# Two of an expert's six weight pieces loaded as one transfer with 32 KB rows

## The chip, the cores and the metric
One core of a Trainium2 chip runs the whole program as one launch. The metric is the device time of an execution in microseconds (us), the lower the better; three executions give a median.

## The reference
A decoder layer for 256 tokens of width 1024, all in float32: RMS norm and a projection, two groups of mixing heads (attention with forgetting, RWKV-7), an output projection, then a mixture of experts, then a gated per-layer input and a last norm. The expert part, cut to what matters here:

```python
logits = xt @ w_router + b_router
top_val, top_idx = lax.top_k(logits, 4)          # 4 of 32 experts for each token
gates = jax.nn.softmax(top_val, axis=-1)
# for each block of tokens that share an expert e:
hh = xb @ w_gu[e] + b_gu[e]                      # 1024 x 2048 weights, 8 MB
glu = jnp.minimum(hh[:, :1024], 7.0)
lin = jnp.clip(hh[:, 1024:], -7.0, 7.0)
act = glu * jax.nn.sigmoid(1.702 * glu) * (lin + 1.0)
out += (act @ w_down[e] + b_down[e]) * gate      # 1024 x 1024 weights, 4 MB
```

## The kernel before
The mixing part takes the first 240 us. After it, the kernel works through items: an item is one expert with up to 64 of its tokens. There are 32 items in this execution (3072 matmul records of line 855 stand for 32 items of 6 pieces of 16 records), numbered 0 to 31; how many there are is known only at run time.

**Pieces.** The weights of an item, 12 MB, are cut into six pieces of 2 MB, each with 128 rows of 16 KB, one row for each partition. Pieces 0 to 3 are the gate and up matrices, pieces 4 and 5 the down matrix. In HBM all lie in one array `we[expert, piece]`. In SBUF there are nine places: `ring` has six slots, one for each piece, and `extra` (the tile B) has three more for pieces 3, 4 and 5 of odd items. So pieces 0 to 2 have one place each, and pieces 3 to 5 have two each, for even and odd items.

**TensorE.** `item` (line 864) runs on TensorE: biases, then `product` for pieces 0, 1, 2, 3, then the scatter of the former item (L832), the gate matrix (L879), transposes of the activation (L899), the gather for item i + 2 (L817), product 4, transposes of gathered tokens (L824), product 5. The next item begins with its biases (L869). `product` (line 844) waits for the landing semaphore of its piece and then issues its matmuls (L855); the last of them counts up `s_used`. So `s_used` is 6 i + q + 1 when piece q of item i has been used.

**SyncE.** It issues every weight load, in the order of its program, on one queue, and waits for `s_used` ahead of each, so that the place is free. `first_item` (L337) loads item 0; lines 364 and 372 load pieces 3 to 5 of item 1, and line 387 its pieces 0 to 2 and pieces 3 to 5 of item 2. Then two loops follow. `ahead` (line 404), for items 2 to 9: pieces 0 to 2 of item i, then pieces 3 to 5 of item i + 1, each once the same piece of item i - 1 has been used. `in_turn` (line 411), from item 10 on: the six pieces of item i in their order, pieces 0 to 2 once item i - 1 has used them, pieces 3 to 5 once item i - 2 has. After item 31 come the gate weights of the tail (`wgate`, L428, two pieces of 2 MB into ring slots 3 and 4) and the final gain.

**The tail** after item 31: a last scatter (L840), transposes (L935), the gate products (L941), activation, norm and the stores.

Of the kernel before, what the change touches and what calls it, by code (L numbers as in the profile page):

```python
# [18 lines left out]
D = 1024  # L19
# [121 lines left out]
def fox_rwkv7_moe_ple(nc, t, out):  # L141
    with ExitStack() as ctx:
# [3 lines left out]
        def sem(name):  # L146
            return ctx.enter_context(nc.semaphore(name))
# [3 lines left out]
        ring = sb("ring", [P, NSLOT, KD * PW])  # L151
# [4 lines left out]
        B = sb("B", [P, 15, D])  # L156
# [103 lines left out]
        s_bt = sem("expert_bias_landed")  # L260
        s_we = [sem(f"expert_piece{q}_landed") for q in range(6)]
        s_odd = [sem(f"odd_expert_piece{q}_landed") for q in range(3, 6)]
        s_ple = sem("layer_projection_landed")
# [8 lines left out]
        s_used = sem("expert_pieces_used")  # L272
# [46 lines left out]
        def _(sp):  # L319
# [7 lines left out]
            for n in range(NSLOT):  # L327
                piece(n, t[f"wz{n}"], ZP[n][1])
                if n == 1:
# [4 lines left out]
                    sp.dma_start(brt[:, :], t["brt"]).then_inc(s_aux, 16)  # L334

            def first_item(q):
                sp.dma_start(ring[:, q, :], t["we"][0, q]).then_inc(s_we[q], 16)  # L337

# [32 lines left out]
            sp.wait_ge(s_dve, dve_at["mix"])  # L371
            sp.dma_start(extra[2], t["we"][1, 5]).then_inc(s_odd[2], 16)
            sp.wait_ge(s_pe, pe_at["xo10"])
# [4 lines left out]

            def place(q, odd):
                return extra[q - 3] if odd and q >= 3 else ring[:, q, :]  # L380

            def landed(q, odd):
                return s_odd[q - 3] if odd and q >= 3 else s_we[q]

            for q in range(6):
                sp.wait_ge(s_used, q + 1)
                sp.dma_start(place(q, q < 3), t["we"][1 if q < 3 else 2, q]).then_inc(landed(q, q < 3), 16)

# [5 lines left out]
            last_pair = pairs + 1  # L394
            EARLY = 4
# [3 lines left out]

            def load(e, q, odd):  # L400
                sp.dma_start(place(q, odd), t["we"][bass.ds(e, 1), q, :, :].rearrange("a p n -> (a p) n"))\
                    .then_inc(landed(q, odd), 16)
# [8 lines left out]
            def in_turn(i, odd, qs=range(6)):  # L411

                e = weights(i)
                for q in qs:
                    sp.wait_ge(s_used, 6 * i + (q - 5 if q < 3 else q - 11))
                    load(e, q, odd)

            with sp.Fori(0, EARLY) as p:
                ahead(2 * p + 2, False)
                ahead(2 * p + 3, True)  # L420
            in_turn(2 * EARLY + 2, False, range(3))
            in_turn(2 * EARLY + 3, True)
            with sp.Fori(EARLY, pairs) as p:
                in_turn(2 * p + 4, False)
                in_turn(2 * p + 5, True)
            for q in range(2):
# [19 lines left out]
        def _(pe):  # L446
# [396 lines left out]

            def product(i, odd, q, bank_, lhs, first):
                weights = extra[q - 3] if odd and q >= 3 else ring[:, q, :]
                w = weights.rearrange("p (k h c) -> p k h c", k=4, h=2)
                if q < 3:
                    pe.wait_ge(s_we[q], 16 * i + 16)
                elif odd:
                    pe.wait_ge(s_odd[q - 3], 8 * i + 8)  # L850
                else:
                    pe.wait_ge(s_we[q], 8 * i + 16)
# [9 lines left out]
            x_of, act_of = half_of(xT), half_of(aT)  # L862

            def item(i, odd, first=False, last=False):
# [17 lines left out]
                for q in range(4):  # L882
                    if last and q == 3:
                        former()
                        gate_matrix()
                    product(i, odd, q, 6 + q // 2, x_of, False)
                    if first and q < 3:
                        (overflow_rows, overflow_places, overflow_tables)[q]()
# [14 lines left out]
                pe.wait_ge(s_aT, i + 1)  # L903
                product(i, odd, 4, 4, act_of, True)
                if not last:
# [14 lines left out]
            last_pair = pairs + 1  # L920
# [806 lines left out]
```

## Time and profile before

| | us |
|---|---|
| median of three executions | 1198.04 |
| lowest and highest | 1197.19 to 1199.14 |
| the profiled execution | 1197.98 |
| its span, first to last instruction | 1196.2 |
| TensorE busy | 1140.5 |
| DMA, time that the packets of the load queue took, share of 16 engines' span | 86.5% |

The profile is of one execution. The span is 1.8 us shorter than the time of that execution. A busy time of TensorE means matmuls in flight, and SyncE (SP) counts as a queue of issues: the row of an issue has its start and how long the issuing took, and how long the transfer took to land stands separately.

### The profile page before, as it was taken

To read this page: it belongs to the slowest core of one execution; us is meant where nothing else is said; L and a number is where in the kernel's file an instruction comes from. 1 tells how busy PE (TensorE), PEld (TensorE's weight loads), DVE (VectorE), ACT (ScalarE), POOL (GpSimd) and SP (SyncE) were. 2 spreads that over 40 slices of the span, in tenths; PEclk is the share of its full clock that TensorE was granted. 3 is DMA by queue.
4 is the path that set the end of the run, shared out by engine and by line. 5 is a ranking of instruction groups with operands and counts; after the bars stand their busy time and mean duration, and the time that the engine had idled before them with its cause. 6 is when DMAs were issued, how large, how long until landed. Compare 5 with 4: busy or idle time off the path is not lost.

```text
span 1196.2 us, 16921 instructions
## 1 busy us (share of the span) xinstructions
PE 1140.5 (95%) x7060; PEld 482.8 (40%) x7060; DVE 282.4 (24%) x576; ACT 173.1 (14%) x319; POOL 0.2 (0%) x4
## 2 busy tenths in 40 slices
PE   7999999999999999999999999999999999999997
PEld 6888866533333333333333333333333333333334
DVE  2455635321111211111211211111111111111123
ACT  3323432210100100000010010000000000000015
POOL 0000000000000000000000000000000000000000
PEclk9999999899999999999999999999999999999999
DMA  9732125579999999999999999999999999999970
GB/s 378 316 141 73 44 101 212 228 292 393 429 427 429 429 428 428 429 428 428 429 428 428 429 428 430 428 428 429 428 428 428 428 429 429 428 428 429 427 332 36
DMA packets 32228, 434.90 MB, mean 364 GB/s; under 512 B 3840, under 2 KB 4096, under 8 KB 5952
## 3 DMA queue, kind: packets, MB, share of 16 engines
q1 hardware_dynamic: 32192, 434.37, 86.5%
q8 instruction: 29, 0.48, 0.2%
q14 instruction: 7, 0.06, 0.0%
HBM read 433.31 MB, written 1.05 MB: 363 GB/s over the span
## 4 chain that ended last, share of the span: by engine, by line
DMA 42%; PE 40%; DVE 1%; issue 0%; ACT 0%; SPq 0%; DVEq 0%
DMA ring<-in_we 42%; PE PS L855 27%; PE PS L941 2%; PE PS L703 2%; PE PS L817 2%; PE PS L832 2%; PE PS L869 1%; PE PS L824 1%; PE PS L753 1%; PE PS L899 0%; PE PS L879 0%; PE PS L759 0%; PE PS L731 0%; PE PS L498 0%; DVE xq L1248 0%
## 5 line engine op out<-in xcount | busy, mean ns | idle before, releaser
L855 PE MATMUL PS<-ring,FV 128*64 128x512 f32 x2304 | 515.4, 596 | 26.1 <-DMA ring<-in_we 26.1
L855 PEld LDWEIGHTS PS<-ring,FV 128*64 128x64 f32 x2304 | 158.0, 137 | 364.6 <-issue 302.1
L855 PE MATMUL PS<-B,FV 128*64 128x512 f32 x768 | 174.0, 595 | 9.4 <-DMA B<-in_we 8.7
L855 PEld LDWEIGHTS PS<-B,FV 128*64 128x64 f32 x768 | 53.0, 137 | 114.4 <-issue 98.6
L486 PE MATMUL PS<-hT,ring 128*128 128x256 f32 x416 | 93.0, 382 | 0.9 <-ACT hT L994 0.7
L486 PEld LDWEIGHTS PS<-hT,ring 128*128 128x128 f32 x416 | 78.1, 190 | 12.3 <-ACT hT L994 0.8
L1475 DVE TENSOR_SCALAR rz<-con,lora 64x64 f32<-64x64 f32 x30 | 7.4, 247 | 306.1 <-PE PS L855 306.1
L1557 DVE TENSOR_SCALAR hT<-PS 128x512 f32<-128x512 f32 x32 | 22.1, 692 | 185.7 <-PE PS L855 185.7
L1248 DVE TENSOR_TENSOR FV<-PS,prm 128x512 f32<-128x512 f32 x32 | 22.1, 692 | 184.6 <-PE PS L824 184.6
L1153 ACT ACTIVATE FV<-PS 128x512 f32<-128x512 f32 x32 | 19.1, 597 | 298.4 <-PE PS L899 298.4
L817 PE MATMUL PS<-xq,rz 128*64 128x512 f32 x256 | 62.0, 605 | 0.0
L832 PE MATMUL PS<-B,rz 64*128 64x512 f32 x248 | 61.6, 615 | 0.0
L1151 ACT ACTIVATE hT<-hT 128x512 f32<-128x512 f32 x32 | 20.1, 630 | 270.2 <-DVE hT L1549 270.2
L1157 ACT ACTIVATE B<-PS 128x512 f32<-128x512 f32 x32 | 19.1, 597 | 224.4 <-PE PS L855 224.4
L832 PEld LDWEIGHTS PS<-B,rz 64*128 64x128 f32 x248 | 21.4, 186 | 39.7 <-issue 39.7
L869 PE MATMUL PS<-FG,rz 32*64 32x512 f32 x256 | 34.8, 612 | 0.9 <-DVE FV L1248 0.9
L941 PE MATMUL PS<-ring,hT 128*128 128x512 f32 (+1 forms) x80 | 28.1, 508 | 0.2 <-DVE hT L1248 0.2
L703 PE MATMUL PS<-ring,hT 128*128 128x512 f32 x64 | 28.1, 592 | 0.0
L1248 DVE TENSOR_TENSOR hT<-hT 128x512 f32<-128x512 f32 x32 | 22.2, 693 | 21.7 <-ACT hT L1151 21.6
L817 PEld LDWEIGHTS PS<-xq,rz 128*64 128x64 f32 x256 | 15.5, 136 | 24.9 <-issue 23.4
L1139 ACT ACTIVATE B<-PS 128x512 f32<-128x512 f32 x32 | 19.1, 597 | 41.5 <-PE PS L817 41.5
L1549 DVE TENSOR_SCALAR hT<-PS 128x512 f32<-128x512 f32 x32 | 21.6, 676 | 10.4 <-PE PS L855 10.4
(264 smaller groups left out, 679.4 us busy)
## 6 DMA issues: line engine op xcount, KB each, us to landing
ring<-in_we SPq DMA_DIRECT2D x144, 2048.0 KB, 24.2
B<-in_we SPq DMA_DIRECT2D x48, 2048.0 KB, 29.3
ring<-in_wz SPq DMA_DIRECT2D x7, 2048.0 KB, 22.7
ring<-in_wo SPq DMA_DIRECT2D x2, 2048.0 KB, 7.9
ring<-in_wgate SPq DMA_DIRECT2D x2, 2048.0 KB, 38.7
xq<-in_x SPq DMA_DIRECT2D x2, 512.0 KB, 5.4
ring<-in_wz SPq DMA_DIRECT2D x1, 1024.0 KB, 8.6
xq<-in_x SPq DMA_DIRECT2D x1, 1024.0 KB, 5.0
```

The lines of the kernel that those rows point to most:

```text
L486: mm = pe.matmul(bank(z_bank(n), SEQ), w[:, k, at:at + P], hT[:, k, :], **flags)
L703: mm = pe.matmul(bank(2 * q + b), mixT[:, k, b * P:(b + 1) * P], w[:, k, :], start=(k == 0), stop=(k == KD - 1))
L817: mm = pe.matmul(PS[64 * h:64 * h + 64, 6, :], PM[:, b, :], xs[:, b, 512 * h:512 * h + 512], start=(b == 0), stop=(b == TB - 1))
L832: mm = pe.matmul(bank(2 * q + b), GTs[rows, b * P:(b + 1) * P], ysb[rows, :], start=False, stop=False, skip_group_check=True)
L855: mm = pe.matmul(PS[64 * h:64 * h + 64, bank_, :], lhs(4 * (q % 2) + k), w[:, k, h, :], start=(first and k == 0), stop=(q % 2 == 1 and k = ...
L869: pe.matmul(PS[64 * h:64 * h + 64, 6 + s, :], OHB[NE * s:NE * s + NE, :], bT[NE * s:NE * s + NE, 512 * h:512 * h + 512], start=True, stop= ...
L941: mm = pe.matmul(PS[:, 2 * q + b if c0 == 0 else 4, 0:c1 - c0], hT[:, k, b * P:(b + 1) * P], w[:, k, c0:c1], start=(k == 0), stop=(k == KD ...
L1139: act.activation(Xg, bank(6), ACT.Copy).then_inc(s_xg, 1)
L1151: act.activation(e_s, e_g, ACT.Sigmoid, scale=SALPHA).then_inc(s_sig, 1)
L1248: return v.tensor_tensor(o, a, b, op)
L1549: v.tensor_scalar(e_g, bank(6), LIMIT, None, ALU.min).then_inc(s_glu, 1)
L1557: v.tensor_scalar(e_l, bank(7), LIMIT, -LIMIT, ALU.min, ALU.max).then_inc(s_vl, 1)
```

## The change
The arrays in HBM are split: `we0`, `we1`, `we2` and `we5` hold one piece each, and `we34` holds pieces 3 and 4 of each expert side by side, so that a row is 32 KB. Where a merged load is made, one transfer of 4 MB fills both places (ring slots 3 and 4, or the first two places of `extra`), on one semaphore. It is issued once piece 4 of the former owner has been used (before, piece 3 waited for piece 3, and piece 4 for piece 4), and product 3 waits for all of it. It is done for item 1 and for items 3 to 30. Items 0 and 2 and the last item keep single transfers (`last_in_turn`), which read half rows of `we34`. For items 0 and 2 pieces 3 and 4 share a semaphore, and product 3 waits for both. The loops keep their order of loads; `in_turn` is split so that the last item stands behind the loop. The core of the diff (the renamed semaphores and the host's concatenation are left out):

```diff
+        extra34 = B[:, 0:8, :].rearrange("p a n -> p (a n)")
...
             sp.wait_ge(s_pe, pe_at[f"y{NC - 1}"])
-            for a in range(2):
-                sp.dma_start(extra[a], t["we"][1, 3 + a]).then_inc(s_odd[a], 16)
+            sp.dma_start(extra34, t["we34"][1]).then_inc(s_odd[0], 16)
...
+            ring34 = ring[:, 3:5, :].rearrange("p a n -> p (a n)")
+            def up(e, i):
+                for q in range(3):
+                    sp.wait_ge(s_used, 6 * i + (q - 5))
+                    sp.dma_start(ring[:, q, :], of(t[f"we{q}"], e)).then_inc(s_up[q], 16)
+            def down(e, i, odd, used):
+                sp.wait_ge(s_used, 6 * i + (used + 5))
+                sp.dma_start(extra34 if odd else ring34, of(t["we34"], e)).then_inc((s_odd if odd else s_down)[0], 16)
+                sp.wait_ge(s_used, 6 * i + (used + 6))
+                sp.dma_start(extra[2] if odd else ring[:, 5, :], of(t["we5"], e)).then_inc((s_odd if odd else s_down)[1], 16)
             def ahead(i, odd):
                 e, e_next = weights(i), weights(i, 1)
-                for q in range(6):
-                    sp.wait_ge(s_used, 6 * i + (q - 5))
-                    load(e if q < 3 else e_next, q, odd == (q < 3))
+                up(e, i)
+                down(e_next, i, not odd, -6)
+            def in_turn(i, odd):
                 e = weights(i)
-                for q in qs:
-                    sp.wait_ge(s_used, 6 * i + (q - 5 if q < 3 else q - 11))
-                    load(e, q, odd)
+                up(e, i)
+                down(e, i, odd, -12)
+            def last_in_turn(i):
+                e = weights(i)
+                up(e, i)
+                for a in range(2):
+                    sp.wait_ge(s_used, 6 * i + (a - 8))
+                    sp.dma_start(extra[a], of(t["we34"][:, :, 4 * D * a:4 * D * (a + 1)], e)).then_inc(s_last4 if a else s_odd[0], 16)
+                sp.wait_ge(s_used, 6 * i - 6)
+                sp.dma_start(extra[2], of(t["we5"], e)).then_inc(s_odd[1], 16)
...
-            in_turn(2 * EARLY + 2, False, range(3))
-            in_turn(2 * EARLY + 3, True)
+            up(weights(2 * EARLY + 2), 2 * EARLY + 2)
             with sp.Fori(EARLY, pairs) as p:
+                in_turn(2 * p + 3, True)
                 in_turn(2 * p + 4, False)
-                in_turn(2 * p + 5, True)
+            last_in_turn(2 * last_pair + 1)
...
                 elif odd:
-                    pe.wait_ge(s_odd[q - 3], 8 * i + 8)
+                    if last and q == 4:
+                        pe.wait_ge(s_last4, 16)
+                    else:
+                        pe.wait_ge(s_odd[q // 5], 8 * i + 8)
```

## Rows read from the trace of the kernel before

**Rows 1.** The page: TensorE, rates in 40 slices of 29.9 us, the chain by engine.
```profile
PE 1140.5 (95%) x7060; PEld 482.8 (40%) x7060; DVE 282.4 (24%) x576; ACT 173.1 (14%) x319; POOL 0.2 (0%) x4
...
GB/s 378 316 141 73 44 101 212 228 292 393 429 427 429 429 428 428 429 428 428 429 428 428 429 428 430 428 428 429 428 428 428 428 429 429 428 428 429 427 332 36
...
DMA 42%; PE 40%; DVE 1%; issue 0%; ACT 0%; SPq 0%; DVEq 0%
```

**Rows 2.** Busy time by stretch; last columns: TensorE clock, DMA share, GB/s.
```profile
400.00:534.00 134.00, 125.67 (x596) 40.64 (x592) 22.58 (x51) 10.84 (x19) 0.00 (x0) 1.00 1.01 428
543.00:690.00 147.00, 147.00 (x712) 49.85 (x712) 27.17 (x61) 13.90 (x23) 0.00 (x0) 1.00 1.01 429
729.00:1136.00 407.00, 381.87 (x1804) 124.59 (x1804) 68.65 (x150) 33.27 (x55) 0.00 (x0) 1.00 1.01 428
```

**Rows 3.** Chain in order of time, items 29 to 31: start, us, what.
```profile
1081.24 25.49 DMA ring<-in_we
1106.77 3.68 PE PS L855 x16
1110.60 25.49 DMA ring<-in_we
1136.13 3.65 PE PS L855 x16
```

**Rows 4.** TensorE in order of time, items 3 to 5: nothing waits for a load.
```profile
337.50 3.60 PE L855 MATMUL PS<-B,FV 128*64 128x512 f32 x16
341.03 1.99 PE L832 MATMUL PS<-B,rz 64*128 64x512 f32 x8
...
354.24 13.96 PE L855 MATMUL PS<-ring,FV 128*64 128x512 f32 x64
...
381.34 10.52 PE L855 MATMUL PS<-ring,FV 128*64 128x512 f32 x48
391.69 0.60 PE L855 MATMUL PS<-B,FV 128*64 128x512 f32 x2
```

**Rows 5.** TensorE in order of time, late items: products 2 and 3 of 30.
```profile
1106.77 3.65 PE L855 MATMUL PS<-ring,FV 128*64 128x512 f32 x16 [0.58 <-DMA ring<-in_we]
1111.67 3.65 PE L855 MATMUL PS<-ring,FV 128*64 128x512 f32 x16 [1.25 <-DMA ring<-in_we]
```

**Rows 6.** Chain of the tail, then issue and landing of the gate weights.
```profile
1148.69 7.09 PE PS L855 x32
...
1161.15 3.67 PE PS L941 x8
...
1192.39 0.75 DVE xq L1615
...
L428 SPq DMA_DIRECT2D ring<-in_wgate x2: 338/342/346, 1115.4 to 1123.4; - x2
...
DMA to landing us min/median/max: 37.2/38.7/40.3
```

**Rows 7.** Packets in 11:12 (16 KB rows), 185:186 (8 KB rows), 600:700; page: x again.
```profile
q1 hardware_dynamic: 24, 0.39, 91.7%
...
q1 hardware_dynamic: 54, 0.44, 104.3%
...
DMA packets 2947, 42.85 MB, mean 428 GB/s; under 512 B 332, under 2 KB 332, under 8 KB 332
...
q1 hardware_dynamic: 2947, 42.85, 100.6%
...
xq<-in_x SPq DMA_DIRECT2D x1, 1024.0 KB, 5.0
```

**Rows 8.** Issues of SyncE, each with its landing, then all loads of weights.
```profile
283.65 0.33 SPq L401 DMA_DIRECT2D ring<-in_we  x1
...
DMA to landing us min/median/max: 15.5/15.5/15.5
...
295.14 0.33 SPq L401 DMA_DIRECT2D B<-in_we  x1
...
DMA to landing us min/median/max: 7.5/24.8/38.4
```

**Rows 9.** Items 13 and 14: issue and landing of a piece 4, TensorE after product 3.
```profile
593.35 0.33 SPq L401 DMA_DIRECT2D B<-in_we  x1
...
DMA to landing us min/median/max: 24.0/24.0/24.0
...
622.47 1.99 PE L832 MATMUL PS<-B,rz 64*128 64x512 f32 x8
```

**Rows 10.** Busy time by stretch, the end of the mixing part.
```profile
229.80:236.60 6.80, 6.80 (x16) 3.54 (x15) 2.18 (x12) 0.54 (x3) 0.00 (x0) 0.50 0.77 325
236.70:245.00 8.30, 7.36 (x37) 2.57 (x38) 3.80 (x17) 2.85 (x4) 0.00 (x0) 1.00 0.00 0
```

More of the change, by code:

```diff
@@ L260, in fox_rwkv7_moe_ple @@
         s_bt = sem("expert_bias_landed")
-        s_we = [sem(f"expert_piece{q}_landed") for q in range(6)]
-        s_odd = [sem(f"odd_expert_piece{q}_landed") for q in range(3, 6)]
+        s_up = [sem(f"expert_piece{q}_landed") for q in range(3)]
+        s_down = [sem("expert_pieces34_landed"), sem("expert_piece5_landed")]
+        s_odd = [sem("odd_expert_pieces34_landed"), sem("odd_expert_piece5_landed")]
+        s_last4 = sem("last_expert_piece4_landed")
         s_ple = sem("layer_projection_landed")
@@ L334, in _, with single @@
                     sp.dma_start(brt[:, :], t["brt"]).then_inc(s_aux, 16)
+            def single(q):
+                if q in (3, 4):
+                    return t["we34"][:, :, (q - 3) * 4 * D:(q - 2) * 4 * D]
+                return t[f"we{q}"]
             def first_item(q):
-                sp.dma_start(ring[:, q, :], t["we"][0, q]).then_inc(s_we[q], 16)
+                sp.dma_start(ring[:, q, :], single(q)[0]).then_inc(s_up[q] if q < 3 else s_down[q // 5], 16)
             def after(n):
@@ L371, in _ @@
             sp.wait_ge(s_dve, dve_at["mix"])
-            sp.dma_start(extra[2], t["we"][1, 5]).then_inc(s_odd[2], 16)
+            sp.dma_start(extra[2], t["we5"][1]).then_inc(s_odd[1], 16)
             sp.wait_ge(s_pe, pe_at["xo10"])
@@ L377, in _ @@
             first_item(5)
[L379 to L383, printed above, removed]
             for q in range(6):
                 sp.wait_ge(s_used, q + 1)
-                sp.dma_start(place(q, q < 3), t["we"][1 if q < 3 else 2, q]).then_inc(landed(q, q < 3), 16)
+                sp.dma_start(ring[:, q, :], single(q)[1 if q < 3 else 2]).then_inc(s_up[q] if q < 3 else s_down[q // 5], 16)
             sp.wait_ge(s_used, 7)
@@ L398, in weights, with of @@
                 return sp.value_load(EI[0:1, bass.ds(i + a, 1)], min_val=0, max_val=NE - 1)
-            def load(e, q, odd):
-                sp.dma_start(place(q, odd), t["we"][bass.ds(e, 1), q, :, :].rearrange("a p n -> (a p) n"))\
-                    .then_inc(landed(q, odd), 16)
+            def of(w, e):
+                return w[bass.ds(e, 1), :, :].rearrange("a p n -> (a p) n")
+            ring34 = ring[:, 3:5, :].rearrange("p a n -> p (a n)")
[8 more added lines that the diff above has]
+                sp.dma_start(extra[2] if odd else ring[:, 5, :], of(t["we5"], e)).then_inc((s_odd if odd else s_down)[1], 16)
             def ahead(i, odd):
                 e, e_next = weights(i), weights(i, 1)
-                for q in range(6):
-                    sp.wait_ge(s_used, 6 * i + (q - 5))
-                    load(e if q < 3 else e_next, q, odd == (q < 3))
-            def in_turn(i, odd, qs=range(6)):
+                up(e, i)
+                down(e_next, i, not odd, -6)
+            def in_turn(i, odd):
                 e = weights(i)
-                for q in qs:
-                    sp.wait_ge(s_used, 6 * i + (q - 5 if q < 3 else q - 11))
-                    load(e, q, odd)
+                up(e, i)
[8 more added lines that the diff above has]
+                sp.dma_start(extra[2], of(t["we5"], e)).then_inc(s_odd[1], 16)
             with sp.Fori(0, EARLY) as p:
@@ L842, in scatter_last, with product @@
                     finish(mm, "tpe", f"s{b}")
-            def product(i, odd, q, bank_, lhs, first):
+            def product(i, odd, q, bank_, lhs, first, last=False, head=False):
                 weights = extra[q - 3] if odd and q >= 3 else ring[:, q, :]
@@ L885, in item @@
                         gate_matrix()
-                    product(i, odd, q, 6 + q // 2, x_of, False)
+                    product(i, odd, q, 6 + q // 2, x_of, False, last, first)
                     if first and q < 3:
@@ L903, in item @@
                 pe.wait_ge(s_aT, i + 1)
-                product(i, odd, 4, 4, act_of, True)
+                product(i, odd, 4, 4, act_of, True, last, first)
                 if not last:
@@ L1712 @@
     dn = a["w_down"][0].reshape(NE, 2, 4, P, D).transpose(0, 1, 3, 2, 4).reshape(NE, 2, P, 4 * D)
-    host["we"] = np.concatenate([gu, dn], 1)
+    for q in range(3):
+        host[f"we{q}"] = gu[:, q]
+    host["we34"] = np.concatenate([gu[:, 3], dn[:, 0]], -1)
+    host["we5"] = dn[:, 1]
     host["bT"] = np.concatenate([a["b_gu"][0][:, 0:FF], a["b_gu"][0][:, FF:]], 0)
```

8 lines of the change are left out of this document (6 added, 2 removed).

## The prediction
> **What bounds the kernel now.** I read the page first, then the stretches, the chain, the two engines in order of time and the packets.
>
> The page shows TensorE busy for 95% of the span and a load rate of 427 to 430 GB/s in nearly every slice from the eleventh to the thirty-eighth [rows 1]. The two bounds lie so close together that the share of busy time doesn't settle which one holds. The stretches do. Between 400 and 534 us and between 729 and 1136 us TensorE is idle for 8.3 and 25.1 us, with the rate at 428 GB/s; between 543 and 690 us it is never idle, at the same rate [rows 2]. So the loads never pause, and TensorE is paced by them in two stretches and runs on stored pieces in between.
>
> The chain says how closely. From one product 2 to the next it holds a load of 25.49 us and a product of 3.68 us, and product 2 starts at 1106.77 and again at 1136.13: 29.36 us an item, 4.893 us for each of six pieces [rows 3]. An item in which TensorE waits for no load takes 27.1 us: two items go by between 337.50 and 391.69 [rows 4]. In the late items the missing 2.3 us are two short waits, each on a piece that has just landed: product 2 (0.58 us) and product 3 (1.25 us), 4.90 us apart [rows 5]; what is left is the restart of weight loads. The last such wait is for piece 2 of item 31, at 1136.13. Behind it the tail is TensorE work, up to 1196.2 with short steps of the other engines [rows 3, 6]. The gate weights have landed by 1123.4 + 37.2 = 1160.6, and the tail takes the first half of them from 1161.15 and the second later, so no load sets the end after 1136.13 [rows 6].
>
> The time to ask for is therefore the start of product 2 of item 31. Whatever moves it by some us moves the end by as much.
>
> **Part 1: the rows of 32 KB.** A load is spread over 16 DMA engines, 8 rows each. With 16 KB rows a packet takes 0.917 x 16 us / 24 = 611 ns, with 8 KB rows 1.043 x 16 us / 54 = 309 ns [rows 7]. Two small packets cost 2 x 309.0 - 611.3 = 6.7 ns more than one of twice the size. No row of 32 KB is in this trace, so the step from 16 to 32 KB is taken to be worth as much: 8 x 6.7 = 54 ns for a merge. One completion less comes on top: 4893 ns for a piece less 8 x 611.3 ns leaves 3 ns. Together 57 ns.
>
> Merges that count are those ahead of the last wait and in the unbroken stretch: items 3 to 30, 28 of them. The gain is 28 x 0.057 = 1.6 us. Bounds: the lone loads are 7.5 us for 16 KB rows [rows 8] and 5.0 us for 8 KB rows [rows 7]. Their difference, 2.5 us over 8 rows, is 312 ns a row, and 300 or 325 ns if both are rounded badly. Taken from 309 ns this leaves +9 to -16 ns for a packet, -3.5 in the middle. I use +9 as the upper end (28 x 75 ns = 2.1 us) and the middle as the lower (a loss of 28 x 25 ns = 0.7 us), and the value from saturated engines, because that is the state of the stretch in question.
>
> The Trainium skill gives another size (DMA: Bandwidth & Descriptors, Bandwidth): each packet has a fixed overhead of about three cycles inside the DMA engine, and the fabric runs at 850 MHz. An estimate from that page is 3.5 ns a packet, 28 ns a merge and 0.8 us in all, by which the sum below would be +3.3 us, not +2.5. The trace has the overhead nearly twice as large.
>
> **Part 2: product 3 waits for piece 4 too.** This is the cost, and it falls on TensorE. Pieces 3 and 4 land together, when piece 4 landed before.
>
> In items 2 to 10 pieces 3 to 5 come an item ahead, so product 3 finds them there. From item 11 on they come in turn. TensorE has stock then: piece 4 of item 13 lands at 593.35 + 24.0 = 617.35, and product 3 of item 13 starts at 622.47 - 3.53 (product 3 to L832 in [rows 4]) = 618.94, 1.6 us later [rows 9]. An item further, loads have moved by 29.36 and TensorE by 27.1 us, so in item 14 it waits for the pair, by 0.7 us, and in every item from there on. Before, it was idle for no load up to 690 us, in item 16 [rows 2].
>
> From item 15 on there is one wait an item, of about 29.36 - 27.1 = 2.3 us at product 3, in place of the two. The pace stays that of the loads. But TensorE now runs later against them, and at the end it can't catch up. The step to item 31:
> - Before, product 3 of item 30 started at 1111.67, when piece 3 had landed [rows 5]. Piece 4 lands one piece later, at 1116.5, so product 3 starts at 1111.67 + 4.89 = 1116.56.
> - From product 3 to the products of the next item it is 354.24 - 337.50 = 16.74 us, and two products more are 2 x 3.45 = 6.90 us (10.35 us for three, 381.34 to 391.69) [rows 4]: 23.64 us.
> - Product 2 of item 31 starts at 1116.56 + 23.64 = 1140.20, where it started at 1136.13 [rows 3]. Its own load had landed by then, so nothing is left of the wait that the chain ended in. The difference is +4.07 us.
>
> That item 31 is loaded in single pieces doesn't help: its piece 3 lands 4.89 us after piece 2 and is there before TensorE comes to it either way (product 3 of item 31 isn't held before).
>
> **Part 3: the issue of the pair is later, and what stands behind it.** SyncE waits for product 4 in place of product 3, and behind that wait stand piece 5 and pieces 0 to 2 of the next item. For piece 5 and those behind nothing changes: piece 4 was issued at that moment before, ahead of them. Only piece 3 comes later, by the 8.0 us between the ends of two products. It costs nothing as long as older loads cover it. The thinnest cover is at the first merge in the loop, item 3: it is issued at 295.14, where piece 4 was. A lone load lands after 7.5 us, and of these 4.9 us are its bytes, so the first byte needs 2.6 us to count: the engines must have work up to 297.8. The load in front was issued at 283.65 and lands at 283.65 + 15.5 = 299.15 [rows 8]. There are 1.4 us of cover, and each later item adds 29.36 - 27.1 = 2.3 us. From item 11 on the pair waits for item i - 2, long done. Cost: nothing.
>
> The loads of pieces 0 to 2 in the late items are issued up to 4 us later, since TensorE frees their slots later; they took 25.49 us to land [rows 3], over 20 us of it in line behind others, so the queue doesn't notice. The same holds for the gate weights, which spent 37 us in line [rows 6]. SyncE has one issue less in an item; it isn't busy.
>
> **Part 4: edits with one answer.** Item 1's pair, half rows of `we34` for items 0, 2 and 31, the shared semaphores of items 0 and 2, and the split of the loop: all these loads land tens of us ahead of use or keep their place in line. Nothing.
>
> **Sum.** 4.07 - 1.60 = +2.5 us on a profiled execution of 1197.98 us (span 1196.2, and 1.8 us around it). This execution is within 0.1 us of the median, so the forecast is 1200.4 us. The bounds of part 1 give +2.0 to +4.8, that is 1199.9 to 1202.8.
>
> **The rivals.**
> 1. *The 32 KB rows aren't moved as such.* If each is cut into two packets of 16 KB, or the saving stops at 16 KB, only the 3 ns of the completion stay, 0.1 us in all, and the lag is paid in full: 4.0 us, 1202.0. Nothing in the trace shows a packet above 16 KB. Against it: the saving from 8 to 16 KB, and that between 600 and 700 us packets are whole rows: 42.85 MB in 2947 - 332 of them [rows 7]. 14%.
> 2. *The lag doesn't reach the end.* If product 3 of item 30 is not the last thing held (the loop has more room than the undisturbed item shows), the gain of the loads passes to the end alone: 1.6 us less, 1196.4. The late rows speak against it: TensorE has 2.3 us to spare in an item, less than the 4.9 us it is held. 6%.
> 3. *The queue runs dry at item 3.* It does if a 4 MB load takes over 4.0 us to start instead of 2.6, or if it is needed by the engine that is done first. I price it at the size of the cover, 1.4 us, in addition: 1201.8. 5%.
> 4. *The clock falls.* Waits of 2.3 us in one piece are longer than any in this stretch, 1.25 us. The granted clock has fallen once on the way, from the full level of 2.4 to 1.2 GHz for 6.8 us [rows 10], without an idle stretch, among many small products. One such fall in the last items costs half of it, 3.4 us: 1203.8. 5%.
> 5. *Each transfer has a cost of its own that a merge saves.* The load would have to wait for the former one to complete. The 28 merges at the 2.6 us by which a lone load is longer than its bytes would bring 73 us: 1125. The spacing of 4.893 us leaves 3 ns for it, so it is overlapped. 1%. The Trainium skill has this as a rule (DMA: Bandwidth & Descriptors, Anatomy of one DMA): about 2 us fixed for a transfer whatever its size, and its advice is to merge.
>
> **How the numbers follow.** 68% for the forecast, 14, 6, 5, 5 and 1 for the rivals, and 1 for what I don't see. A measurement of this kernel can tell about 0.2% from no change, 2.4 us, so the line is at 1200.4 and my forecast stands on it. Of its 68% I give slower 33 and same 35, since gains somewhat above 57 ns are as likely as gains below. With rivals 1, 3 and 4 slower has 57%, with rival 2 same has 41%, and faster has 2%. The range reaches from 1199.0, below which are rival 2 and 5, to 1202.8, which takes in rival 1 and the bounds of the gain; rival 4 is outside.
>
> **What the profile after would show.** Packets of 32 KB at about 1216 ns, six pieces in 29.30 us instead of 29.36, and 4,176 packets fewer (29 merges by 128 + 16). One wait of some 2 us at product 3 in each of the items 15 to 30, none at product 2 there. Product 2 of item 31 starts at 1138.6, without a wait, and the gate weights land by 1159. From there to the end 60.1 us as before. I would be wrong if product 2 of item 31 still waited for its load, if packets stayed at 16 KB, or if the rate fell below 428 GB/s around 300 us.

## The result, and the profile after

| | before | after |
|---|---|---|
| median, same chip, seven executions each (us) | 1198.04 | 1203.37 |
| lowest and highest | 1195.46 to 1199.92 | 1201.67 to 1204.46 |
| the profiled execution | 1197.98 | 1202.98 |
| its span | 1196.2 | 1201.2 |
| TensorE busy | 1140.5 | 1149.2 |
| packets | 32228 | 28051 |

The ratio is 1.0047, with a 95% interval from 1.0035 to 1.0059. The changed kernel is slower by 5.3 us. The forecast had the right sign and half the size, and the result lies above its range.

The page of the profile after, to be read beside [rows 1]:

```profile
PE 1149.2 (96%) x7060; PEld 486.6 (41%) x7060; DVE 282.3 (24%) x576; ACT 173.1 (14%) x319; POOL 0.2 (0%) x4
...
GB/s 371 319 140 74 37 108 211 228 304 378 431 428 430 429 431 430 429 424 429 430 430 428 429 431 429 430 430 432 429 432 429 428 431 428 432 429 428 424 256 35
DMA packets 28051, 434.89 MB, mean 362 GB/s; under 512 B 3376, under 2 KB 3632, under 8 KB 5488
...
PE 49%; DMA 33%; DVE 0%; SPq 0%; issue 0%; ACT 0%; DVEq 0%
```

The loads are a little faster, as the change meant them to be: many slices of 430 to 432 GB/s, where nearly all were 427 to 429. But the chain has moved from DMA (42% before, 33% after) to TensorE (40% before, 49% after). TensorE is busy for 8.7 us more with the same 7060 matmuls, and those can only be slower matmuls.

TensorE in order of time, one row each from items 14, 16, 29 and 30 and two from item 31. Here L883 is `product`; the bracket is the wait ahead of it:

```profile
647.07 3.65 PE L883 MATMUL PS<-ring,FV 128*64 128x512 f32 x16 [0.23 <-DMA ring<-in_we]
...
705.65 5.35 PE L883 MATMUL PS<-ring,FV 128*64 128x512 f32 x16 [1.96 <-DMA ring<-in_we]
...
1086.48 3.65 PE L883 MATMUL PS<-B,FV 128*64 128x512 f32 x16 [0.28 <-DMA B<-in_we]
...
1115.79 5.35 PE L883 MATMUL PS<-ring,FV 128*64 128x512 f32 x16 [1.98 <-DMA ring<-in_we]
...
1134.28 10.52 PE L883 MATMUL PS<-ring,FV 128*64 128x512 f32 x48
...
1153.71 7.09 PE L883 MATMUL PS<-B,FV 128*64 128x512 f32 x32 [0.69 <-ACT FV L1181]
```

In place of the two waits of [rows 5] there is one at product 3. It begins in item 14 (0.23 us) and is about 2 us later on. Products 0 to 2 of item 31 run in one go from 1134.28, so product 2 starts at about 1141.2 (forecast 1138.6) and waits for no load. What was not forecast is in the second column: product 3 of item 30 takes 5.35 us where it took 3.65. The stretches around it (columns as in [rows 2]: the last three are TensorE clock, DMA share, GB/s):

```profile
1112.60:1115.97 3.37, 1.39 (x8) 0.33 (x6) 0.17 (x1) 0.00 (x0) 0.00 (x0) 1.00 0.90 384
1115.97:1119.38 3.41, 3.41 (x10) 0.99 (x10) 0.00 (x0) 0.00 (x0) 0.00 (x0) 0.50 1.04 442
1119.40:1122.80 3.40, 3.40 (x16) 0.98 (x12) 1.38 (x2) 0.00 (x0) 0.00 (x0) 1.00 0.97 414
```

The granted clock is 0.50 for 3.41 us, that is 1.2 GHz in place of 2.4, just after the wait. TensorE had been idle for 1.98 us and was at work again for 0.2 us when it fell. This happens in product 3 of seven items between 705 and 1119 us. In the execution before, no stretch between 240 and 1190 us shows it.

**Where the 5.0 us of the span are.** The last piece that TensorE is held by in item 30 is piece 4 in the changed kernel. I follow from its landing to the start of product 4 of item 31, the first product after which nothing differs (1148.69 in [rows 6], 1153.71 above):

| | before | after | difference |
|---|---|---|---|
| piece 4 of item 30 has landed | 1116.52 | 1115.74 | -0.78 |
| from there to product 4 of item 31 | 32.17 | 37.97 | +5.80 |
| product 4 of item 31 starts | 1148.69 | 1153.71 | +5.02 |

The second line is a lag of 4.1 us and a clock term of 3.41 / 2 = 1.7 us; the experiments separate them. The first line is the gain of the rows less something lost on the way. The pairs of items 14 and 30 landed just ahead of 647.07 and 1115.79, 16 items apart: 29.295 us an item, where it was 29.36 [rows 3]. That is 66 ns a merge; over all pairs the landings give 68 ns and 28 x 0.068 = 1.9 us. So 1.9 - 0.8 = 1.1 us was lost, all of it by the last load of item 4.

**The start of the loop.** Issue and landing of piece 2 of item 2 and of the pair of item 3, one view for each:

```profile
L409 SPq DMA_DIRECT2D ring<-in_we x1: 333/333/333, 283.5 to 283.5; - x1
...
DMA to landing us min/median/max: 15.6/15.6/15.6
...
L413 SPq DMA_DIRECT2D B<-in_we x1: 333/333/333, 295.1 to 295.1; - x1
...
DMA to landing us min/median/max: 14.3/14.3/14.3
```

The load in front landed at 299.1 and the pair at 309.35 (unrounded), 10.26 us later, where two pieces in line take 9.72. So 0.53 us was lost there. The other part is 0.75 us at piece 5 of item 4, which landed at 344.30 where 343.55 was due. There only one of the 16 engines was late, with an instruction packet moved beside the loads at 340.5. (The two make 1.28; the load in front had landed 0.1 us earlier than in the kernel before, and the rest is rounding.)

The forecast named a load rate below 428 GB/s around 300 us as a sign of being wrong. It came. The same five microseconds in the kernel before and in the changed one:

```profile
295.00:300.00 5.00, 5.00 (x28) 1.54 (x27) 1.73 (x5) 0.60 (x1) 0.00 (x0) 1.00 1.01 433
...
295.00:300.00 5.00, 5.00 (x28) 1.50 (x27) 1.74 (x5) 0.60 (x1) 0.00 (x0) 1.00 1.01 360
```

### The profile page after: what moved, and what is told of

Its sections match the earlier page's. It is cut to its first block, busy times and chain, and to the rows that moved or that the text cites. A ratio compares the mean times of both kernels' runs of the same rounds, so it can differ in the third digit from the quotient of the medians.

```text
span 1201.2 us, 16749 instructions
## 1 busy us (share of the span) xinstructions
PE 1149.2 (96%) x7060; PEld 486.6 (41%) x7060; DVE 282.3 (24%) x576; ACT 173.1 (14%) x319; POOL 0.2 (0%) x4
## 2 busy tenths in 40 slices
DMA packets 28051, 434.89 MB, mean 362 GB/s; under 512 B 3376, under 2 KB 3632, under 8 KB 5488
## 4 chain that ended last, share of the span: by engine, by line
PE 49%; DMA 33%; DVE 0%; SPq 0%; issue 0%; ACT 0%; DVEq 0%
PE PS L883 34%; DMA ring<-in_we 33%; PE PS L838 3%; PE PS L853 3%; PE PS L969 2%; PE PS L724 2%; PE PS L897 2%; PE PS L845 1%; PE PS L927 1%; PE PS L907 1%; PE PS L774 0%; DMA hT<-in_wproj 0%; PE PS L780 0%; PE PS L519 0%; SPq L409 0%
## 5 line engine op out<-in xcount | busy, mean ns | idle before, releaser
L883 PE MATMUL PS<-ring,FV 128*64 128x512 f32 x2304 | 521.2, 604 | 21.4 <-DMA ring<-in_we 21.4
L883 PEld LDWEIGHTS PS<-ring,FV 128*64 128x64 f32 x2304 | 161.1, 138 | 362.3 <-issue 319.2
L883 PE MATMUL PS<-B,FV 128*64 128x512 f32 x768 | 177.5, 605 | 9.8 <-DMA B<-in_we 9.1
L883 PEld LDWEIGHTS PS<-B,FV 128*64 128x64 f32 x768 | 53.7, 139 | 117.7 <-issue 100.6
```

## The experiments

All ratios are to the kernel before, run beside each kernel on the same chip, with a 95% interval in brackets. The first question was which part of the change costs the time: the added wait, the issue, or the rows.

### The wait alone

The kernel before with all its single loads, and one wait more in `product`:

```diff
+                if q == 3:
+                    if odd:
+                        pe.wait_ge(s_odd[1], 8 * i + 8)
+                    else:
+                        pe.wait_ge(s_we[4], 8 * i + 16)
```

> The kernel before, with all its 2 MB transfers and its semaphores, in which product 3 of every item waits for the landing of piece 4 as well. Nothing of the rows, the packets or the issues changes. Theory 'lag and clock': TensorE is held once an item, about 2.0 to 2.3 us at product 3, from item 14 on; product 2 of item 31 starts 4.07 us later than in the kernel before, and 1.70 us more if a stretch at half clock (3.4 us) falls behind the wait of item 30. Time 4.1 or 5.8 us above the kernel before, and about as long as the changed kernel or up to 1 us longer, since the gain of the rows is missing. Several stretches of 3.4 us at half clock. Rival 'the rows or the later issue cost it': within 1 us of the kernel before, no half clock.

Median 1203.63 beside 1197.99, ratio 1.0043 [1.0027, 1.0060]. TensorE in order of time at item 30:

```profile
1116.75 5.35 PE L860 MATMUL PS<-ring,FV 128*64 128x512 f32 x16 [2.04 <-DMA ring<-in_we]
```

The stretch of the fall, columns as above:

```profile
1118.00:1121.40 3.40, 3.40 (x10) 1.20 (x8) 0.00 (x0) 0.00 (x0) 0.00 (x0) 0.50 1.02 434
```

The wait alone costs as much as the whole change, with no merged transfer and no moved issue in the program: the gain of the rows (1.9 us) is missing, and so is most of what the changed kernel lost on the way (1.1 us). It brings the same wait of 2 us and the same fall of the clock, so the fall doesn't need 32 KB rows. From the landing of piece 4 of item 30 (1116.61) to product 4 of item 31 (1154.67) it is 38.06 us, as in the changed kernel (37.97).

### The wait in one item

The same wait in item 30 alone:

```diff
-            item(2 * last_pair, False)
+            item(2 * last_pair, False, hold=True)
...
+                if hold and q == 3:
+                    pe.wait_ge(s_we[4], 8 * i + 16)
```

> The kernel before, in which product 3 waits for piece 4 as well in item 30 alone: one added wait in the whole program. Theory 'the lag is made at the last held item': the whole of 4.07 us is there, 5.8 us if the clock falls behind this wait, in which case one stretch of 3.4 us at half clock starts near 1117 us. Rival 'the lag builds up over the twenty items that are held': 0.3 us or less.

Median 1203.95, ratio 1.0043 [1.0029, 1.0057]. TensorE in order of time, item 30 and product 4 of item 31:

```profile
1118.58 5.87 PE L857 MATMUL PS<-ring,FV 128*64 128x512 f32 x16 [6.23 <-DMA ring<-in_we]
...
1157.02 7.09 PE L857 MATMUL PS<-B,FV 128*64 128x512 f32 x32 [0.69 <-ACT FV L1155]
```

The stretch of the fall:

```profile
1116.25:1123.08 6.83, 4.50 (x12) 1.58 (x14) 0.00 (x0) 0.00 (x0) 0.00 (x0) 0.50 1.00 425
```

One wait in the last held item costs as much as one in each of 17. The wait is 6.23 us long, about 1.25 + 4.89, since TensorE hadn't fallen behind before. From the landing (1118.45) to product 4 of item 31 it is 38.6 us: the 32.17 of before, 4.1 of lag, and 2.2 of a fall that lasts 6.83 us and of which 4.50 lie in matmuls. The lag is made once, at the end, whatever happens earlier. This execution was the longest of the five (1206.28 us): its loads were 1.9 us behind those of the kernel before, though both programs load alike. 1.5 us of that was lost at piece 5 of item 4, where the changed kernel lost 0.75.

### Single loads at the end

The changed kernel, with items 27 to 31 loaded in single pieces:

```diff
-            last_in_turn(2 * last_pair + 1)
+            for k in range(LATE):
+                last_in_turn(2 * full + (2 * k + 3), True)
+                last_in_turn(2 * full + (2 * k + 4), False)
+            last_in_turn(2 * full + (2 * LATE + 3))
```

> The changed kernel with the last five items (27 to 31) in single pieces instead of the last alone. Theory 'lag and clock': TensorE makes up 2.26 us in each item that isn't held at product 3, so the lag (4.07 us, or 5.77 with a fall of the clock in item 26) is gone before item 31, and falls of the clock in the items up to 26 cost nothing. Product 2 of item 31 starts on the landing of its own piece again. Left are the gain of the rows, 24 x 0.066 = 1.6 us, and what the loads lost around 300 us (about 1.1 us in the profiled run of the changed kernel): 0.3 to 1.6 us below the kernel before. Rival 'the pair as such is slow, wherever it stands' (32 KB rows, or each fall of the clock paid in full, 1.7 us seven times): at least 3 us above the kernel before.

Median 1198.03 beside 1197.99, ratio 0.9993 [0.9984, 1.0003]. TensorE at item 31:

```profile
1136.02 3.65 PE L888 MATMUL PS<-ring,FV 128*64 128x512 f32 x16 [1.38 <-DMA ring<-in_we]
```

Product 2 of item 31 waits for its own load again, so the end goes back to the loads and the loss is gone. Five falls of the clock between 735 and 998 us cost nothing: TensorE makes them good out of its next wait. What the remaining 24 merges should have brought, 1.6 us, doesn't come out whole; the interval leaves room for none to 1.9 us. In the profiled execution single landings were late by 1.4 us in all, 0.80 of them at the very piece 2 of item 31 that product 2 waits for (an instruction packet stands at 1133.8).

### The clock's share

Four unused matmuls ahead of product 3 in items 18 to 30 of the changed kernel, so that TensorE isn't idle while it is held:

```diff
+                    if fill and q == 3:
+                        for _ in range(4):
+                            pe.matmul(PS[:, 5, 256:512], ident, xs[:, 0, 0:256], start=True, stop=True)
```

> The changed kernel with four matmuls of 128x256, of which nothing is used, ahead of product 3 in items 18 to 30: about 1.8 us of work in the place where TensorE waits 2.0 to 2.3 us. Theory 'clock': no stretch at half clock after item 18, waits of 0.2 to 0.5 us in every one of these items, and the end 1.7 us earlier than in an execution of the changed kernel that has a fall in item 30: about 3.4 us above the kernel before in place of 5. Rival 'the clock falls for another reason, or its fall costs nothing at the end': falls stay, or the time is that of the changed kernel or above it.

Median 1203.24, ratio 1.0039 [1.0026, 1.0052]. In the profile the falls are gone and product 4 of item 31 starts at 1152.32, 1.4 us earlier than in the changed kernel. The ratio is hardly lower than that kernel's (1.0047); the 3.4 us expected lie inside its interval too. Part of the gain was lost elsewhere: the first pair of the loop came 1.31 us late here, not 0.53. Inconclusive by the times.

So I took the start of the loop out as well. First, pairs only from item 11 on:

```diff
-                down(e_next, i, not odd, -6)
+                down_single(e_next, i, not odd)
```

> The changed kernel with items 3 to 10 in single pieces, each issued when its own place is free; the pairs are left from item 11 to 30. Theory 'the first pairs of the loop drain the queue': without them the loads around 300 us are as in the kernel before (piece 2 of item 2 to the end of item 3 spaced by 4.89 us), and the loss of about 1.1 us is gone while 8 x 0.066 = 0.5 us of gain is missing: 0.6 us below the changed kernel. Rival 'that loss was chance, not the pair': the landings around 300 us show it here as well, and the time is 0.5 us above the changed kernel. Lag and falls of the clock stay either way.

Median 1202.07, ratio 1.0038 [1.0025, 1.0051]. Nothing is lost at item 3 (pieces 4.9 us apart), but 0.67 us is at piece 5 of item 4, which is loaded as in the kernel before. Piece 4 of item 30 lands at 1114.76, a whole us ahead of the changed kernel; 0.94 of it was there at piece 2 of item 2 already, before any load of the two differs. The 0.6 us that this run was to gain doesn't show in the times. In its profiled execution (1200.34 us) the clock happened not to fall in item 30. TensorE, items 29 to 31:

```profile
1085.51 5.35 PE L897 MATMUL PS<-B,FV 128*64 128x512 f32 x16 [1.98 <-DMA B<-in_we]
...
1114.80 3.65 PE L897 MATMUL PS<-ring,FV 128*64 128x512 f32 x16 [0.28 <-DMA ring<-in_we]
...
1151.02 7.09 PE L897 MATMUL PS<-B,FV 128*64 128x512 f32 x32 [0.69 <-ACT FV L1198]
```

At its end this execution runs as the forecast described. That it took 1200.34 us, the very time forecast, is luck: it had 20 merges and not 28, lost 0.67 us at item 4, and its loads were 1.0 us ahead of the kernel before at the start. The lag is 1151.02 - 1114.76 = 36.26 us against 32.17, that is 4.09. The first two rows also show how a fall hides: the one in item 29 makes TensorE 1.7 us later, and the next wait is 0.28 instead of 1.98. Only one in item 30, with no wait behind it, reaches the end.

Then the same with the unused matmuls (from item 18 on):

> Pairs in items 11 to 30 (no pairs at the start), with the four unused matmuls ahead of product 3 in items 18 to 30. Theory 'clock': no half clock after item 18, product 2 of item 31 starts 23.7 us after the pair of item 30 has landed, in every execution: 4.07 - 1.3 = 2.8 us above the kernel before; the same pairs without the fill end 1.7 us later whenever the clock falls in item 30, and are as fast when it doesn't (its profiled execution). Rival 'the clock isn't what makes those executions longer': median as without the fill, 4 us above the kernel before.

Median 1200.88 beside 1197.8, ratio 1.0024 [1.0014, 1.0035]. The same stretch of the changed kernel:

```profile
740.00:1190.00 450.00, 431.82 (x1953) 147.05 (x1950) 80.14 (x170) 49.81 (x91) 0.00 (x0) 0.98 0.94 401
```

That of this one:

```profile
740.00:1190.00 450.00, 449.02 (x2073) 165.84 (x2070) 81.55 (x173) 51.03 (x94) 0.00 (x0) 1.00 0.94 400
```

And TensorE of this one at product 4 of item 31:

```profile
1151.23 7.09 PE L897 MATMUL PS<-B,FV 128*64 128x512 f32 x32 [0.69 <-ACT FV L1204]
```

With neither the falls nor the loss at the start, 2.9 us are left: the lag less the gain of 20 merges, forecast at 2.8. Its interval touches the changed kernel's own (1.0035 to 1.0059) at one end. Against the run before it (1.0038), the intervals overlap. So that the clock costs 1.7 us is shown by the profiled executions, and the times only lean that way.

### Is there a gain to keep?

Next I tried to keep the gain of the rows without the lag: pairs of 3 and 4 in items 11 to 26 alone, and triples of pieces 3 to 5 (rows of 48 KB) in items 11 to 24. In the second:

```diff
+        MERGED = (3, 4, 5)
...
+                sp.wait_ge(s_used, 6 * i + (max(MERGED) - 11))
+                sp.dma_start(whole[odd], t["weM"][bass.ds(e, 1), :, :].rearrange("a p n -> (a p) n")).then_inc(landed(3, odd), 16)
```

> Pairs in items 11 to 26 only; items up to 10 and 27 to 31 in single pieces, as in the kernel before. Theory 'lag and clock, and a drained queue at the first pairs': no loss around 300 us, product 2 of item 31 starts on the landing of its piece, falls of the clock up to item 26 cost nothing. Left is the gain of 16 pairs, 16 x 0.066 = 1.1 us: 0.1% below the kernel before, and 0 to 1 us below the kernel with pairs from item 3 and five single items at the end. Rival 'a fall of the clock or a pair costs wherever it stands': at least 2 us above the kernel before.

> As the former, with pieces 3, 4 and 5 in one transfer with rows of 48 KB in items 11 to 24 and the last seven items in single pieces. Theory: each item gains twice 0.066 us, 14 x 0.132 = 1.8 us in all; TensorE lags 9.8 us at item 24 and makes up 2.26 us in each of six items and more, 13.6 us, so nothing of it is left: 1.8 us (0.15%) below the kernel before, packets of 49152 B at about 1820 ns. Rival 'the step above 32 KB brings nothing, or longer waits hold the lag': no gain beyond the 1.0 us of the pairs, or product 2 of item 31 late.

Both missed. Medians 1198.17 and 1198.12 beside 1197.8, ratios 1.0002 [0.9993, 1.0011] and 0.9999 [0.9989, 1.0009]. The merges worked: a packet of 48 KB took 1819 ns, and the lag was gone. But some loads came late in the profiled executions, by 1.06 and 0.53 us in the first and by 0.34, 1.06 and 0.45 us in the second. Each time it was one engine of the 16, 1.5 to 1.7 us behind its rhythm, and an instruction packet had been moved up to 6.3 us before. TensorE's loop is cut and partly unrolled in both, and they fetch 37 and 39 instruction packets where the kernel before fetches 29.

Hence a run with that code and nothing else: the kernel before, its loads and waits, with items 10, 11 and 26 to 29 unrolled.

```diff
-            with pe.Fori(0, pairs) as p:
+            with pe.Fori(0, 4) as p:
...
+            item(10, False)
+            item(11, True)
+            with pe.Fori(5, full) as p:
```

> The kernel before with every load, wait and matmul as it was; only TensorE's program is written differently: its loop over items is cut in two, and items 10, 11 and 26 to 29 stand outside the loops. In the two kernels with such a program (pairs or threes in the middle items) six packets of 16 KB of instructions more fell into the stretch of the loads, and the landing next to several of them was 0.3 to 1.1 us late. Theory 'code fetched beside the loads delays them': more instruction packets after 500 us than the kernel before has, single landings late by 0.3 to 1.1 us while the first engine's share of them is on time, and 0.5 to 1.5 us more than the kernel before. Rival 'it was something else about these kernels': within 0.3 us of the kernel before.

Median 1199.83 beside 1198.39, ratio 1.0010 [1.0001, 1.0019]. This code costs 1.2 us by the ratio, 1.4 by the medians; the interval reaches from 0.1 to 2.3 us. It fetches 37 instruction packets. The packets in one microsecond, 1048 to 1049, ahead of a late landing (queue, packets, MB, share of 16 engines):

```profile
q1 hardware_dynamic: 31, 0.43, 100.1%
q8 instruction: 1, 0.02, 6.4%
```

TensorE in order of time, the product 2 that waits for this load:

```profile
1050.61 3.65 PE L855 MATMUL PS<-ring,FV 128*64 128x512 f32 x16 [1.78 <-DMA ring<-in_we]
```

One packet of 16 KB of code takes 6.4% of 16 engine-microseconds, 1.02 us, of one engine. Fifteen engines end this load by 1049.38, on time, and the last at 1050.56, 1.2 us late; the load lands with it, and product 2 waits 1.78 us instead of 0.58. The next load is as late (1055.31), so the delay stays.

Not every such packet delays a landing, and the landings show why. A load lands with 16 events, one from each engine. Set against those of the load in front, 4.89 us later, fifteen keep their time and one is late by 1.4 to 1.6 us. That is so at ten of the twelve packets of 16 KB that this execution has between 300 and 1150 us (at the other two, at 540 and 566 us, several engines are late at once), and beside such packets in the other executions. So each packet of code sets one engine back by about 1.5 us. The trace doesn't name a packet's engine, but nothing else stands there. The landing is late only if that engine is among the last already: by 1.2 and 0.5 us at two of the packets that this code adds, by nothing at the others. In the execution of the kernel before, the packet at 340.6 made one engine 1.6 us late as well (342.77 for 341.18), and piece 5 of item 4 landed on time, at 343.24, with another engine.

The late landings of the two runs above, 1.6 and 1.9 us in all, are of this kind and of the size of the gains that they missed (1.1 and 1.8 us); how the delays spread over their other executions isn't shown. The runs with single loads at the end, with unused matmuls or with pairs from item 11 on have two to four instruction packets more than the kernel before; by an estimate from this run (1.2 us for eight) that is 0.3 to 0.6 us in each.

### Pieces 4 and 5 in place of 3 and 4

The pair whose second half is used soonest after the first: product 5 follows product 4 directly, but for a short transpose. Loops as in the changed kernel, 28 merges.

```diff
+            def pair(e, odd):
+                sp.dma_start(both[odd], t["we45"][bass.ds(e, 1), :, :].rearrange("a p n -> (a p) n")).then_inc(landed(4, odd), 16)
```

> The changed kernel with another pair: pieces 4 and 5 (the down matrix) in one transfer with rows of 32 KB in items 3 to 30, piece 3 by itself. Theory: product 4 of item 30 waits until piece 5 has landed (1121.4 without the gain of rows); from product 4 to product 2 of the next item it is 361.1 - 345.5 = 15.6 us, so product 2 of item 31 starts 0.95 us later than in the kernel before, in place of 4.07. With the gain of 28 x 0.066 = 1.85 us the sum is -0.9 us, or +0.8 us where the clock falls in item 30. No drained queue at the first pair, since piece 3 of item 3 is issued at 287 us as before. Rival 'a pair costs 4 us or more wherever it stands in the item': time of the changed kernel.

Median 1197.35 beside 1198.39, ratio 0.9992 [0.9981, 1.0004]. The late part as a stretch:

```profile
740.00:1190.00 450.00, 425.45 (x1954) 148.63 (x1950) 81.72 (x174) 50.93 (x96) 0.00 (x0) 1.00 0.94 400
```

TensorE in order of time, the held product of item 30 and product 4 of item 31:

```profile
1120.08 3.65 PE L881 MATMUL PS<-ring,FV 128*64 128x512 f32 x16 [1.57 <-DMA ring<-in_we]
...
1148.28 7.09 PE L881 MATMUL PS<-B,FV 128*64 128x512 f32 x32 [0.69 <-ACT FV L1182]
```

The clock stays at 1.00 with waits of 1.57 us, the first pair of the loop lands on time, and product 4 of item 31 starts 0.4 us before [rows 6] has it. From the landing of piece 2 of item 2 to that of piece 5 of item 31 the loads take 849.70 us, 851.55 in the kernel before: 1.85 us less for 28 merges, the whole gain of the rows. The median is 1.0 us below that of the kernel before, as expected (0.9), but the interval takes in 1: a gain isn't shown. Its ratio is the lowest of all versions, hardly below that of single loads at the end (0.9993).

With the unused matmuls added:

> The former with four unused matmuls of 128x256 ahead of product 4 in items 18 to 30. Theory 'clock': no half clock after item 18 and 0.9 us below the kernel before, up to 1.7 us below the former. Rival: as the former or above it.

Median 1198.72, ratio 0.9997 [0.9988, 1.0006]: no better, as its rival had it. There was no fall left to save, and the program has two instruction packets more.

### The changed kernel again

The changed kernel, unaltered:

> The changed kernel once more, unaltered, beside the three others on the same chip. Theory: 5 us above the kernel before, product 2 of item 31 25.4 us after the landing of the pair of item 30 if the clock falls there, 23.7 us if not, and a first engine about 1 us late at the first pair of the loop (item 3).

Median 1202.54 of nine, ratio 1.0031 [1.0021, 1.0041]. That is 3.7 us, 2.5 to 4.9, where 5 was expected: a narrow miss, though the intervals of both measurements overlap. In its profiled execution (1204.80 us) the clock fell in item 30 again:

```profile
1117.62 5.35 PE L883 MATMUL PS<-ring,FV 128*64 128x512 f32 x16 [1.99 <-DMA ring<-in_we]
```

The pair of item 3 was 1.29 us late here, and piece 5 behind it another 1.53 (an instruction packet stands at 314.4). Item 3 is a pair of pieces 3 and 4 in four of the profiled executions, and in all four the first engine to end that pair was 0.9 to 1.2 us late. How late the pair landed varies: 0.14 us with single loads at the end, 0.53 in the changed kernel, 1.29 here, 1.31 with the filled wait. In the ten other profiled executions pieces 3 to 5 of item 3 landed within 0.13 us of their time.

## Why the prediction was right or wrong

**What bounds it: right.** The time of the kernel before was decided at the start of product 2 of item 31. With the single loads at the end it waits for its load again and the loss is gone.

**Part 1, the rows: mechanism right, size a little low.** Packets of 32 KB, four microseconds in which nothing else is moved:

```profile
DMA packets 54, 1.77 MB, mean 442 GB/s; under 512 B 0, under 2 KB 0, under 8 KB 0
...
q1 hardware_dynamic: 54, 1.77, 102.7%
```

That is 1.027 x 64 us / 54 = 1217 ns, forecast 1216. Two of 16 KB cost 2 x 611.3 - 1217 = 5.6 ns more, forecast 6.7; a merge brings 68 ns in the landings, forecast 57, a little more than this difference gives (8 x 5.6 = 45 ns). The bytes went in whole rows (4,177 packets fewer, forecast 4,176), and rival 1 is out. The estimate of 3.5 ns a packet, from the three cycles of the Trainium skill (DMA: Bandwidth & Descriptors, Bandwidth), is below what was measured here too. Rival 5 is out: a merge in a full queue saved 0.07 us. The 2 us for each transfer of the Trainium skill (same page, Anatomy of one DMA) are given there for transfers issued by GpSimd, and mostly as the time that completion takes; no run here has such a transfer, and in SyncE's full queue nothing like it was saved.

**Part 2, the lag: right.** Forecast 4.07 us, measured 4.09 where the clock didn't interfere. The waits begin in item 14, there is one in an item from then on, and product 2 of item 31 waits no more, all as forecast. The wait in item 30 alone shows that the last one makes all of the lag. Rival 2 is out.

**Part 3, the issue of the pair: this step failed.** It was put at nothing and measured 0.5 us (0.1 to 1.3 in other executions). I set the cover against the landing of the load in front, 299.15, which is when its last engine is done. The engines don't end a load together: in the changed kernel the first was done with that load 2.4 us before the last, at 296.7, while the pair, by the working of Part 3, needed until about 297.7. With the cover counted for the first engine it is negative by 1 us. The pair's first packets took up to 2.5 us in place of 1.2, and its first engine was 1.2 us late. Rival 3 named this ("needed by the engine that is done first") and had 5%; it was the case, at less than its price on this execution. The runs with single loads, or with pieces 4 and 5 paired, at item 3 lose nothing there, which agrees.

The 0.75 us at piece 5 of item 4 isn't the change's. The same landing was 0.39 to 1.51 us late in four runs that load item 4 in single pieces (1.51 with the wait in item 30 alone, whose loads are those of the kernel before), and on time in others. The instruction packet near 340 us is in every execution, the kernel before included, and whether the landing suffers depends on the engine that it meets. That the profiled execution of the kernel before was spared is chance.

**Rival 4, the clock: the other step that failed.** The sum has no term for it, and the rival had 5% and 3.4 us. All three profiled executions that wait 2 us in item 30 with TensorE idle have a fall there, at 1.7 us (in a fourth, with pairs from item 11, a fall in item 29 had cut that wait to 0.28 us): a fall lasts 3.41 us, not the 6.8 of the one example [rows 10], and half of that is lost. The reason I gave for doubting it, that the one fall in the trace came without an idle stretch, was no evidence about idle stretches; the longest wait for a load in that part was 1.25 us [rows 5], so it could say nothing of 2 us. A chance near a half would have been fair.

**The sum.** Forecast -1.6 + 4.07 = +2.5. Measured on the profiled executions: -1.9 (rows) + 1.1 (0.5 of it the issue at item 3, the rest chance) + 4.1 (lag) + 1.7 (clock) = +5.0. The two terms that I had at zero, the issue and the clock, are the error, with 0.6 us of chance on top. Both were among the rivals, each alone and with a small chance, and they came together. The range also left out that executions of one kernel differ: those of before in the first comparison go from 1195.5 to 1199.9, and the second measurement of the changed kernel gave 3.7 us where the first gave 5.3.

## What to carry to other kernels

A merged load gives its gain in every item but makes its consumer wait for all of it, and in a stretch paced by loads that delay is paid once, at the last item held: merge the pieces that are used back to back, and keep the last items single. Even so no version run here is shown to be faster than the kernel before. Before a wait is lengthened ask what TensorE's clock does after a wait of that length; where the trace has none so long, the question is open, and 5% is too little for it. Count the cover of a queue for the engine that is done first, and the landing of a load for the one that is done last.

## What the runs showed of the hardware

**The clock after a short wait.** The changed kernel has ten waits of 1.95 to 1.99 us at product 3 between 676 and 1116 us. Seven of them brought 3.4 us at 1.2 GHz, and in the item after such a fall the wait is about 0.3 us. The other three kept 2.4 GHz, as this one (TensorE in order of time):

```profile
822.83 3.65 PE L883 MATMUL PS<-ring,FV 128*64 128x512 f32 x16 [1.97 <-DMA ring<-in_we]
```

Waits of 1.25, 1.38, 1.57 and 1.78 us brought no fall in the profiles above. One of 6.23 us brought 6.83 us at 1.2 GHz, from 3.9 us into the wait on. Length alone doesn't decide: in the run of the triples, waits of 1.89 to 1.93 us in nine items and one of 2.98 us brought none, while one of 2.25 us did. Two of them:

```profile
710.39 3.65 PE L878 MATMUL PS<-ring,FV 128*64 128x512 f32 x16 [1.92 <-DMA ring<-in_weM]
...
945.25 3.65 PE L878 MATMUL PS<-ring,FV 128*64 128x512 f32 x16 [2.98 <-DMA ring<-in_weM]
```

What decides between two like waits stays open.

**Code is loaded by the same engines as the weights.** A packet of 16 KB of instructions takes 1.0 us of one engine, and beside a full queue it set one of the 16 back by about 1.5 us. The landing of the load was late by 0.3 to 1.5 us where that engine was among the last, and on time where it wasn't. The kernel with eight such packets more was slower by 1.2 us (1.0010 [1.0001, 1.0019]). In this stretch bound by loads unrolling had a price, though the same matmuls and loads were executed.

**The first and the last of the 16 engines don't end a load together.** They were 2.4 us apart in the load in front of the first pair (1.6 in the one before it), and 4.2 at 1050 us in the run of the code alone. So a queue can be dry for one engine while the load in front hasn't landed.
